# The low part of peer_up computed by VectorE instead of GpSimd

## What is computed

```python
def block(args):
    xb, idb, gb = args
    a = jnp.einsum('tkd,td->tk', expert_down[idb], xb)
    act = jax.nn.gelu(a.astype(jnp.float32), approximate=False).astype(xb.dtype) * gb
    return jnp.einsum('tk,tkd->td', act, expert_up[idb])
```

## Time and profile before

| | |
|---|---|
| Median of 3 runs | 1828.79 us (1828.55 to 1829.47) |
| Span of the profiled execution | 1829.3 us |
| PE busy | 1639.3 us, 90% |
| VectorE (DVE) busy | 1419.3 us, 78% |
| GpSimd (POOL) busy | 960.6 us, 53% |
| ScalarE (ACT) busy | 666.4 us, 36% |
| DMA | 372.40 MB, 204 GB/s over the span |

### The profile page before, as it was taken

How to read it: one execution, slowest core, us unless ns; L and a number is a source line. 1 busy time by engine, 2 the same in 40 slices (tenths; PEclk the granted TensorE clock), 3 DMA queues, 4 the chain that set the end, 5 groups by cost and what they waited for, 6 DMA issues and landing times.

```text
span 1829.3 us, 29796 instructions
## 1 busy us (share of the span) xinstructions
PE 1639.3 (90%) x8710; PEld 1397.8 (76%) x8710; DVE 1419.3 (78%) x2797; ACT 666.4 (36%) x1138; POOL 960.6 (53%) x845
## 2 busy tenths in 40 slices
PE   4999987661887599999999999999999999999995
PEld 4565456551766588999998888988988899898894
DVE  6555259997997288888888887888888788887888
ACT  2034233334999223333333333333333333332332
POOL 0000106555997166666666556666655666556664
PEclk9999998885999799999999999999999999999998
DMA  9923201100067877777777777777777777777774
GB/s 318 382 99 128 57 12 58 46 22 1 23 186 239 261 251 245 254 241 256 245 252 248 242 243 245 249 241 249 249 246 242 249 244 245 246 250 247 242 250 141
DMA packets 186507, 372.40 MB, mean 204 GB/s; under 512 B 19752, under 2 KB 103280, under 8 KB 186480
## 3 DMA queue, kind: packets, MB, share of 16 engines
q1 hardware_dynamic: 149088, 237.57, 37.9%
q0 software_dynamic: 36864, 134.23, 25.0%
q10 hardware_dynamic: 528, 0.26, 0.0%
HBM read 344.76 MB, written 27.26 MB: 203 GB/s over the span
## 4 chain that ended last, share of the span: by engine, by line
PE 57%; DVE 9%; DMA 9%; issue 6%; ACT 4%; POOL 1%; SPq 1%; DVEq 0%; ACTq 0%; POOLq 0%
PE bank L1522 8%; PE bank L1523 8%; PE bank L1524 8%; PE bank L1536 8%; PE bank L1535 8%; DMA down<-in_peer_down 8%; PE bank L1534 8%; PE bank L1514 5%; PE bank L1493 3%; ACT stage L776 2%; DVE topi L1048 1%; DVE top L1045 1%; DVE cand L1070 1%; DVE pick L1063 1%; DVE score L1052 1%
## 5 line engine op out<-in xcount | busy, mean ns | idle before, releaser
L541 POOL TENSOR_TENSOR ulo<-up,uhi 128x1024 fp32r<-128x1024 f32 x128 | 362.6, 2833 | 296.8 <-ACT uhi L808 296.7
L1522 PE MATMUL bank<-h2hi,dhi 128*128 128x384 f32 x1024 | 355.5, 347 | 0.0
L1165 DVE TENSOR_TENSOR y<-y,bank 128x512 f32<-128x512 f32 x384 | 252.3, 681 | 118.6 <-PE bank L1536 116.3
L1523 PE MATMUL bank<-h2lo,dhi 128*128 128x384 f32 x1024 | 344.1, 336 | 0.0
L1524 PE MATMUL bank<-h2hi,dlo 128*128 128x384 f32 x1024 | 343.9, 336 | 0.0
L1536 PE MATMUL bank<-uhi,alo 128*128 128x512 f32 x768 | 302.4, 394 | 0.0
L1535 PE MATMUL bank<-ulo,ahi 128*128 128x512 f32 x768 | 301.8, 393 | 0.0
L1534 PE MATMUL bank<-uhi,ahi 128*128 128x512 f32 x768 | 299.3, 390 | 2.4 <-DVE alo L1203 2.4
L1174 DVE SCALAR_TENSOR_TENSOR junk<-rows_d,h2nat 128x1024 f32<-128x1024 f32 x128 | 285.3, 2229 | 19.2 <-DVE y L1186 14.9
L814 ACT ACTIVATE ahi<-acts 128x384 fp32r<-128x384 f32 x128 | 67.2, 525 | 634.7 <-DVE acts L1201 634.7
L1523 PEld LDWEIGHTS bank<-h2lo,dhi 128*128 128x128 f32 x1024 | 193.9, 189 | 0.0
(11 more groups left out here) (201 smaller groups left out, 2566.2 us busy)
## 6 DMA issues: line engine op xcount, KB each, us to landing
down<-in_peer_down SPq DMA_DIRECT2D x128, 512.0 KB, 6.2
up<-in_peer_up SPq DMA_DIRECT2D x128, 512.0 KB, 3.4
ada<-in_w_ada SPq DMA_DIRECT2D x12, 2048.0 KB, 16.3
gate<-gates_dram SPq DMA_DIRECT2D x128, 192.0 KB, 5.4
gates_dram<-stage SPq DMA_DIRECT2D x2, 8192.0 KB, 30.4
wq<-in_peer_query SPq DMA_DIRECT2D x16, 512.0 KB, 3.9
gates_dram<-stage SPq DMA_DIRECT2D x4, 2048.0 KB, 10.5
w_in_sb<-in_w_in SPq DMA_DIRECT2D x2, 2048.0 KB, 20.4
```

What stands on the lines that cost most here:

```text
L541: gp.tensor_tensor(ulo[g][s][:], up[s][:], uhi[g][s][:].bitcast(F32), ALU.subtract).then_inc(pool_ulo, 1)
L1165: ve.tensor_tensor(part, part, bank[4 + (OUTS * g + q) % 4][:], ALU.add).then_inc(dve_y, 1)
L1522: pe.matmul(bank[2 + s][:, 0:TD], dhi[s][:, k, :], h2hi[:, k, 0:TD], start=k == 0, stop=False)
L1523: pe.matmul(bank[2 + s][:, 0:TD], dhi[s][:, k, :], h2lo[:, k, 0:TD], start=False, stop=False)
```

## The change

The subtraction `ulo = up - uhi` moves from GpSimd to VectorE, where it stands behind `alo` in each tile and signals `dve_ulo` instead of `pool_ulo`. VectorE gets one more wait in front of it, for `act_uhi`. SP and PE wait for `dve_ulo` where they waited for `pool_ulo`. GpSimd keeps the index copies and the gathers.

```diff
@@ block.sync, turn
-                    sp.wait_ge(pool_ulo, n + 1)
+                    sp.wait_ge(dve_ulo, n + 1)
                     load_up(n + 2, s)
                     sp.wait_ge(dve_act, n + 1)
                     load_gate(n + 2, s)
@@ block.gpsimd
-            def split_up(n, k):
-
-                gp.wait_ge(act_uhi, n + 1)
-                g, s = k // 2, k % 2
-                gp.tensor_tensor(ulo[g][s][:], up[s][:], uhi[g][s][:].bitcast(F32), ALU.subtract).then_inc(pool_ulo, 1)
-
...
                     gather(rows_d, peer_down, idx_d, n, k).then_inc(rows_d_in[k], 16)
-                    if not first:
-                        split_up(n, k)
-
-            for k in range(4):
-                split_up(k, k)
+
             for q in range(4):
                 gp.wait_ge(stored_part[q], 16)
@@ block.vector, tile
                 ve.wait_ge(act_ahi, n + 1)
                 ve.tensor_tensor(alo[g][s][:], acts[s][:], ahi[g][s][:].bitcast(F32), ALU.subtract).then_inc(dve_alo, 1)
+                ve.wait_ge(act_uhi, n + 1)
+                ve.tensor_tensor(ulo[g][s][:], up[s][:], uhi[g][s][:].bitcast(F32), ALU.subtract).then_inc(dve_ulo, 1)
@@ block.tensor, group_ready
                 pe.wait_ge(dve_alo, 2 * i + 2)
-                pe.wait_ge(pool_ulo, 2 * i + 2)
+                pe.wait_ge(dve_ulo, 2 * i + 2)
```

More of the change, by code:

```diff
@@ L332, in build_block @@
             sem(n) for n in ("dve_half", "dve_top", "dve_pair", "dve_sel", "dve_bsub", "dve_pick", "dve_hot"))
-        dve_dlo, dve_act, dve_alo, dve_y = (sem(n) for n in ("dve_dlo", "dve_act", "dve_alo", "dve_y"))
+        dve_dlo, dve_act, dve_alo, dve_ulo, dve_y = (
+            sem(n) for n in ("dve_dlo", "dve_act", "dve_alo", "dve_ulo", "dve_y"))
         dve_ids, dve_dot, dve_coef, dve_add, dve_normed = (sem(n) for n in ("dve_ids", "dve_dot", "dve_coef", "dve_add", "dve_normed"))
-        pool_wq, pool_off, pool_hit, pool_hot, pool_own, pool_ulo, pool_idx, pool_x1, pool = (
-            sem(n) for n in ("pool_wq", "pool_off", "pool_hit", "pool_hot", "pool_own", "pool_ulo", "pool_idx", "pool_x1", "pool"))
+        pool_wq, pool_off, pool_hit, pool_hot, pool_own, pool_idx, pool_x1, pool = (
+            sem(n) for n in ("pool_wq", "pool_off", "pool_hit", "pool_hot", "pool_own", "pool_idx", "pool_x1", "pool"))
         block = ctx.enter_context(nc.Block())
```

## The result

The changed kernel takes 1860.5 us (median of 4 runs, 1857.08 to 1861.91) against 1829.13 us, a ratio of 1.0167 with a 95% interval of 1.0153 to 1.0181. I had forecast 1818.3 us: the sign is wrong. The time is inside the range I gave, and the mechanism is the first of my rivals.

What follows compares the result with a forecast made beforehand. The prediction took PE to bound the kernel, with the down load right behind it. Loop -12.2, start +0.5 and end +1.2 made -10.5 us from a median of 1828.79, so 1818.3 us, with a range of 1811 to 1890.

Steps and rivals of the forecast that it cites:

- the first of my rivals: SP's queue behind dve_ulo: the down load becomes the bound, 1902 us to about 2045 us; chance 0.30.
- What bounds the kernel now: Loop over the expert tiles: PE bounds it, the down load right behind; PE loses 0.12 us a tile, some 14 us.
- The reason given for the late load: VectorE's dot stood still behind GpSimd's subtraction, 3.44 us against 1.23, delaying gate products and then the next down load.
- (a) to (c): GpSimd loses 128 subtractions, VectorE gains them at 1224 ns, dots give back 1.00 us a tile; PE stays the bound.
- (a): GpSimd loses 128 subtractions of 2.4 to 3.3 us, in itself worth nothing since GpSimd is not the bound.
- (d): SP's queue: up, gate and down leave together; down lands at +8.4 to +9.0, wanted at +9.17, margin 0.2 to 0.8 us.
- The rival's formula: Loss per tile if down becomes the bound: +0.6 us at a 5.0 us landing, +1.8 at 6.2.
- (e): Start of the loop: stores of gates move behind ulo, the first gathers come sooner; +0.5 us, bounds -4 and +4.
- (f): End, after the 128th gate products: one more subtraction on VectorE's path, +1.2 us, hidden by nothing.
- The sum: Whole kernel: loop -12.2, start +0.5, end +1.2, together -10.5 us, giving 1818.3 us.

Runs made afterwards that it cites:

- e9: The kernel before the change, with SP sending the up load last, one buffer turn later: 1830.61 us, ratio 0.9980.
- e1: The changed kernel, with SP sending gate and down first and the up load behind them: 1816.45 us, ratio 0.9925 to the kernel before.
- e4: The changed kernel, with VectorE computing ulo behind dlo, early in the tile: 1815.65 us, ratio 0.9899 to the kernel before.
- e12: The changed kernel with ulo behind dlo, run once more beside the changed kernel: 1816.44 us, ratio 0.9895 to the kernel before.
- e5: The changed kernel without gathers from the fifth tile on: 1850.55 us, ratio 1.0117 to the kernel before.
- e2: The changed kernel, with GpSimd waiting for the dot before both gathers, so they start later: 1882.15 us, ratio 1.0295 to the kernel before.
- e3: The kernel before the change, with SP also waiting for alo before up, so up, gate and down leave together: 1867.27 us, ratio 1.0183.
- e11: The changed kernel run again unaltered, as the level of its group: 1859.76 us, ratio 1.0133 to the kernel before.
- e7: The changed kernel, with ScalarE issuing the up load on its own queue and SP only gate and down: 1856.74 us, ratio 1.0124 to the kernel before.

## Why the prediction was wrong, step by step

*What bounds the kernel now:* PE, with the down load right behind it, is right. The reason given for the late load is not, for the most part. The slow dot at 1236.95 can't have delayed a load issued at 1235.12; in 19 of the 23 late tiles it was the landing that was long, beside the gathers (e9, above).

*(a) to (c), VectorE and GpSimd:* the arithmetic is right. The subtraction takes 1.22 us, the dots fell to 1226 ns, VectorE's busy time stayed (164.50 of 200 us), and e1 and e4 show that the 12 to 13 us I expected are there once the loads are in time: 9.19 forecast; 9.187 (e1), 9.167 and 9.187 (e4, e12) measured. That this came out to 0.02 us is partly luck, as I expected it of VectorE's punctuality alone and put GpSimd's freedom at nothing in (a). The trace gives most of it to the gathers, which that freedom moves away from the down load.

*(d), the landing of down:* here the forecast failed, by terms of this step's sum. The issue times held to 0.15 us. The transfer I put at 3.2 to 3.8 us by two rates, one of a long queue of loads at full flow, one of the middle of a burst. Both leave out how a burst begins and how it dips between its loads; alone it takes 4.3 us (e5), and with the gathers beside it a little more. The first bytes come a little sooner than I had it, 1.0 us after the issue of up in e5 and not 1.2 (my row too has bytes from 1232.0 on, 0.9 us after the issue, not from 1232.25), and the 0.4 us to the semaphore holds (1212.74 to 1213.10 there). That moves the landing from +8.4 to +9.0 up to +9.1 to +9.5. And PE wants it at +8.97, not at +9.17, since the transposes start 0.20 us ahead of the mark from which I counted. The margin I claimed was 0.2 to 0.8 us, so it was gone. The pacing of GpSimd I had read wrongly as well: the first gather follows add_up, 0.4 to 1.3 us earlier than I had it, and its bytes meet the end of the load. e5 puts that at 0.05 us a tile. I had chosen the favourable end of a bound whose other end I could name; the row nearest in kind would have been a burst of the same three loads from a standstill, and there was none.

The rival's formula, 4.9 plus the landing less 9.29, gives +0.2 a tile with the measured 4.6, and measured is +0.17. That is close by luck. It counts all of a load's lateness in every tile, where the trace has half: the last partial result of a tile comes 9.41 us after the transposes at the tile's start, and the transposes that need the load sent behind this result start 9.53 us after it, both on average in the changed kernel from 700 to 1780 us. Together that is two tiles, so half of it, 9.47, is the tile. In e5 they are 9.41 and 9.44, half 9.42, and in e2 9.41 and 9.87, half 9.64; measured are 9.421 and 9.632. So 0.1 us beyond the margin costs about 6 us over the loop and not 12, and for landings of 5.0 and 6.2 us the same sum would give about +0.4 and +1.0 a tile (an estimate from these figures), where the prediction has +0.6 and +1.8.

*(e), the start:* +0.5 forecast. Up to the 6th gate products, where the forecast's loop begins, it is +0.2 measured, but another +5.9 falls in the tiles 6 to 9, which the forecast took at 9.19 us like all others. I saw that the gathers would come sooner and counted only what it saved. GpSimd, no longer held by its subtraction, caught up: it began 11 gathers between 653 and 678 us (6 before), and the down load issued beside them was 3.4 us late. The first of these gathers in GpSimd's timeline:

```profile
653.01 1.15 POOL L542 DMA_INDIRECT rows_d<-in_peer_down,idx_d  x1 [0.77 <-POOL idx_d L540]
```

SP's issue of that load:

```profile
663.01 0.33 SPq L408 DMA_DIRECT2D down<-in_peer_down  x1
```

PE, waiting for it, the answer to the second of the earlier trace rows:

```profile
669.57 1.09 PE L1507 MATMUL bank<-ident,down 128*128 128x128 f32 x8 [3.37 <-DMA down<-in_peer_down]
```

Without the gathers (e5) the stretch from 6 to 9 takes 28.3 us, with down sent sooner (e1, e4) 28.1 to 28.8, and with a late burst but GpSimd still held by its subtraction (e3) 28.0, so it takes both, the late burst and the crowd.

*(f), the end:* +1.2 forecast, +2.0 measured. The subtraction is 1.2 of it: the last 36 matmuls wait for ulo, 3.58 us where they waited 2.39 before. The rest is the clock: PE, after that wait, runs more of them at the lower level, and VectorE then waits for a partial result at 1834.89. 12 of the 36 take over 0.6 us, where it was 7. In e1 the wait is the same 3.58 us, 7 are slow, and the end is 30.3. PE's timeline, the first of the last matmuls:

```profile
1829.33 0.76 PE L1527 MATMUL bank<-uhi,ahi 128*128 128x512 f32 x1 [3.58 <-issue]
```

VectorE's:

```profile
1834.89 0.69 DVE L1156 TENSOR_TENSOR y<-y,bank 128x512 f32<-128x512 f32 x1 [0.68 <-PE bank L1529]
```

The windows view of these 16 us, with the granted clock as the third number from the end:

```profile
1826.00:1842.00 16.00, 10.92 (x36) 8.49 (x36) 13.98 (x19) 4.00 (x7) 2.21 (x2) 0.79 0.20 64
```

The mean is 0.79 of the 2.4 GHz level here and 0.89 in the 16 us of the kernel before that begin as long before its 128th gate products. With ulo out of this place (e4) the end is 29.3.

*The sum* was -12.2, +0.5, +1.2. In its own terms it became +26.1 for the 121 tiles from the 6th (9.507 us each against 9.291), +0.2 and +2.0; of the +26.1, 20.2 lie behind the 9th tile.

## What to carry to other kernels

An instruction that moves to another engine moves every wait on its semaphore too: ask of each in-order queue that waits for it what leaves behind it, and when. Here the arithmetic fitted easily and the loads behind one wait of SP did not; the same instruction a few places earlier in the tile turned a loss of 1.7% into a gain of 1%. An engine that is freed matters too, even one that bounds nothing: it issues its own transfers at another time. And a margin of some tenths of a us that rests on a transfer rate is no margin, unless the rate is from a burst of that size and from a standstill.

One order was not tried: the buffer of a down load is free after the transposes at the tile's start, some 13 us before the changed kernel sends the load, which waits in SP's queue for that tile's ulo.

## What the runs showed of the hardware

A burst of 0.52 + 0.20 + 0.52 MB with nothing beside it took 4.3 us, a mean of 289 GB/s (e5), while SP's queue kept up 387 over long loads. A load's time to landing says little by itself: the median was 5.0 us in the kernel where PE never waited for it (e1) and 4.6 where it waited all the time (e11). Moving a load to ScalarE's queue gave the load behind it nothing (e7).

GpSimd's subtraction and VectorE's dot, both with two operands in SBUF, did not run together at all. Between 700 and 1780 us of the kernel before all 116 dots meet a subtraction, and whichever begins first runs through: the subtraction takes 2.40 us and the dot 3.44 when the subtraction is first; the other way round the dot takes its 1.23 us at 1227.56 and the subtraction gets longer, in GpSimd's timeline:

```profile
1227.74 3.31 POOL L541 TENSOR_TENSOR ulo<-up,uhi 128x1024 fp32r<-128x1024 f32 x1 [2.83 <-ACT uhi L808]
```

VectorE's instructions with an operand in a bank went on beside it at their 0.68 us.
